# Two weight chunks of the first projection group are split on ScalarE and VectorE instead of GpSimd

## The reference

```
x = x + sincos_2d(SEQ)
sh1, sc1, gt1, sh2, sc2, gt2 = adaln(c, ada_w, ada_b)         # silu(c) @ ada_w + ada_b, also for c_ctx
hc = modulate(rms_norm(ctx, norm1_g), csh1, csc1)             # h * (1 + scale) + shift
hx = modulate(rms_norm(x, norm1_g), sh1, sc1)
... = hx @ w_in, hc @ w_in                                    # 12 chunks of 512 columns
```

## Time and profile before

| | |
|---|---|
| median of 3 runs | 2148.82 us (2142.51 to 2149.39) |
| profiled execution, span from first to last instruction | 2142.0 us |
| TensorE busy (matmul) | 2005.6 us, 94% |
| VectorE busy | 724.0 us, 34% |
| ScalarE busy | 594.7 us, 28% |
| GpSimd busy | 385.9 us, 18% |
| mean granted TensorE clock | 0.964 of full |
| loaded from HBM | 426.07 MB, 199 GB/s over the span |

### The profile page before, as it was taken

How to read it: one execution, slowest core, us unless ns; L and a number is a source line. 1 busy time by engine, 2 the same in 40 slices (tenths; PEclk the granted TensorE clock), 3 DMA queues, 4 the chain that set the end, 5 groups by cost and what they waited for, 6 DMA issues and landing times.

```text
span 2142.0 us, 27488 instructions
## 1 busy us (share of the span) xinstructions
PE 2005.6 (94%) x11518; PEld 1431.7 (67%) x11518; DVE 724.0 (34%) x1201; ACT 594.7 (28%) x921; POOL 385.9 (18%) x183
## 2 busy tenths in 40 slices
PE   7799989999999999998999798999999899889998
PEld 2567787775444444446887646777777678579998
DVE  1523154323222222226343614222222535533333
ACT  2413112022222222223113414222332311534443
POOL 2400000000000000005003012333343010414653
PEclk9899978989999999999999899999999999998999
DMA  9268914447999999982224003344334232413450
GB/s 358 96 244 295 369 51 160 160 158 305 425 428 419 426 421 427 423 358 105 100 79 150 1 30 138 138 143 171 137 137 140 78 106 94 157 52 145 158 187 29
DMA packets 120207, 428.28 MB, mean 200 GB/s; under 512 B 5690, under 2 KB 23141, under 8 KB 107456
## 3 DMA queue, kind: packets, MB, share of 16 engines
q1 hardware_dynamic: 118016, 416.56, 50.5%
q0 software_dynamic: 2112, 10.57, 1.4%
HBM read 426.07 MB, written 1.05 MB: 199 GB/s over the span
## 4 chain that ended last, share of the span: by engine, by line
PE 70%; PEld 5%; DVE 4%; issue 3%; ACT 3%; POOL 2%; PEldq 0%; DVEq 0%; ACTq 0%
PE bank L505 68%; PEld bank L505 5%; PE bank L520 1%; DVE H L1805 0%; DVE X L2344 0%; POOL arena L1723 0%; POOL arena L1722 0%; DVE arena L2288 0%; POOL arena L1727 0%; PEldq L494 0%; POOL arena L1725 0%; DVE H_low L1812 0%; POOL arena L1728 0%; DVE H L2260 0%; DVE ring_low L2158 0%
## 5 line engine op out<-in xcount | busy, mean ns | idle before, releaser
L505 PE MATMUL bank<-arena_r 128*128 128x512 f32 (+1 forms) x1920 | 560.7, 357 | 40.3 <-DVE H_low L1812 20.8
L505 PE MATMUL bank<-arena_r,ring_low 128*128 128x512 f32 (+2 forms) x1792 | 567.0, 349 | 20.5 <-DVE H_low L1812 17.5
L505 PEld LDWEIGHTS bank<-arena_r 128*128 128x128 f32 x1920 | 342.9, 192 | 138.9 <-issue 56.0
L505 PEld LDWEIGHTS bank<-arena_r,ring_low 128*128 128x128 f32 (+1 forms) x1792 | 333.5, 191 | 67.5 <-issue 21.8
L505 PE MATMUL bank<-arena 128*128 128x64 bf16 (+9 forms) x2684 | 329.3, 291 | 24.7 <-DMA arena<-in_hy_filt_w 11.9
L505 PEld LDWEIGHTS bank<-arena 128*128 128x128 bf16 (+4 forms) x2684 | 210.5, 141 | 128.1 <-issue 90.9
L505 PE MATMUL bank<-ring,arena 128*64 128x512 f32 x1024 | 278.2, 595 | 1.1 <-ACT arena L1423 0.7
L2344 DVE SCALAR_TENSOR_TENSOR X<-bank,mod,X 128x256 f32<-128x256 f32 x216 | 96.4, 481 | 394.0 <-PE bank L505 394.0
L505 PE MATMUL bank<-H_low,arena_r 128*128 128x512 f32 (+1 forms) x608 | 208.0, 342 | 0.0
L1749 POOL TENSOR_TENSOR ring_low<-ring,arena_r 128x2048 fp32r<-128x2048 f32 x32 | 146.6, 4603 | 118.5 <-ACT arena_r L1611 118.5
L1271 ACT ACTIVATE arena<-bank 128x512 f32<-128x512 f32 (+2 forms) x106 | 52.4, 496 | 413.5 <-PE bank L505 413.2
(11 more groups left out here) (263 smaller groups left out, 1908.0 us busy)
## 6 DMA issues: line engine op xcount, KB each, us to landing
ring<-in_moe_w_gate SPq DMA_DIRECT2D x32, 2048.0 KB, 13.7
ring<-in_w_mlp SPq DMA_DIRECT2D x32, 2048.0 KB, 8.3
ring<-in_w_in SPq DMA_DIRECT2D x26, 2048.0 KB, 8.8
ring<-in_ada_w SPq DMA_DIRECT2D x24, 2048.0 KB, 11.8
ring<-in_moe_w_up SPq DMA_DIRECT2D x17, 2048.0 KB, 9.2
H<-in_moe_w_down SPq DMA_DIRECT2D x16, 2048.0 KB, 16.1
arena<-in_moe_w_up SPq DMA_DIRECT2D x15, 2048.0 KB, 9.5
ring<-in_moe_w_down SPq DMA_DIRECT2D x15, 2048.0 KB, 16.3
```

Of the source, the lines that this page charges most:

```text
L505: ins = nc.tensor.matmul(o, l, r, start=start, stop=stop, skip_group_check=True)
```

## The change

GpSimd no longer splits anything in the first phase. Chunk win(0): ScalarE makes the high half in two copies of 2048 columns, after `ada_rows(2)` and before `ada_rows(3)`, and raises `first_high`; VectorE makes the low half in two subtractions, after `take_chunk(0, 2)` and before `take_chunk(0, 3)`, and raises `first_low`, for which TensorE waits at k = 0 and 4. Chunk win(1): VectorE splits it with `split_first(1)`, whole, at the start of the phase "projected", that is after the norm; TensorE waits for it before j = 1. The other edits renumber what is counted on `pool_ready` and `w_split`.

```diff
--- before.py
+++ after.py
@@ -617,10 +617,8 @@
 
                 wide = 2 * L if c in (1, 2) else L
                 if j < 4:
-                    if j == 1:
-                        pe.wait_ge(S("pool_ready"), 8)
-                    elif j:
-                        pe.wait_ge(S("w_split"), j - 1)
+                    if j:
+                        pe.wait_ge(S("w_split"), j)
                     wh, wl = W0h[j % 2].rearrange("p (k n) -> p k n", k=KT), as_cols(n, slot=low)
                 else:
                     chunk_in(n)
@@ -629,7 +627,7 @@
                     for k in range(KT):
                         pe.wait_ge(S("h_split"), k + 1)
                         if k % 4 == 0:
-                            pe.wait_ge(S("pool_ready"), 2 + k // 2)
+                            pe.wait_ge(S("first_low"), k // 4 + 1)
                         for nt in range(2):
                             t = slice(nt * P, (nt + 1) * P)
                             mm3(o[nt], (wh[:, k, t], wl[:, k, t]), (Hp[:, k, :], Hl[:, k, :]), k == 0, k == KT - 1,
@@ -894,7 +892,7 @@
                     for tb in range(TB):
                         mm(ps[2 * tb + nb], PICK[:, tb * P:(tb + 1) * P], YSl[:, s], False, False)
 
-            pe.wait_ge(S("pool_ready"), 9)
+            pe.wait_ge(S("pool_ready"), 1)
             pe.wait_ge(S("onehot"), 1)
             gather(0, 7, "gathered")
             pe.wait_ge(S("hg_ready"), 1)
@@ -950,7 +948,7 @@
                 pe.wait_ge(S("squares"), 8 * 3 + k + 1)
                 mm(ps[0][:, 0:L], ones, H[:, k, 0:L], k == 0, k == KT - 1)
                 if k == 0:
-                    pe.wait_ge(S("pool_ready"), 10)
+                    pe.wait_ge(S("pool_ready"), 2)
                 mm(ps[1][:, 0:L], FIN2[:, k, :], H[:, k, 0:L], k == 0, k == KT - 1, "sum_ready" if k == KT - 1 else None)
             phase_end(pe, "experts")
 
@@ -1193,7 +1191,7 @@
                             for a in range(2):
                                 ada(n, 7 + i, 7, 2 * u + a, 4, ADA_COLS, turns)
                                 n += 1
-                        pe.wait_ge(S("w_split"), 2 + 8 * l + j + 1)
+                        pe.wait_ge(S("w_split"), 3 + 8 * l + j + 1)
 
                         for nt, ks in [(0, (0, 1, 2)), (1, (0, 1, 2)), (0, (3,)), (1, (3,))] + [(t, (0, 1, 2, 3)) for t in range(2, KT)]:
                             if ks[0] == 0:
@@ -1293,8 +1291,14 @@
             mean_root(0, 2 * L, 4, RS0)
             act.wait_ge(S("lb_arg"), 1)
             A_(lbc[:, 8:24], lbc[:, 8:24], ACT.Exp).then_inc(S("lb_exp"), 1)
-            for i in range(1, 4):
+            for i in range(1, 3):
                 ada_rows(i, 6 + i % 2, i % 2)
+            n = win(0)
+            act.wait_ge(full[n % RING], arrived(n))
+            for a in range(2):
+                s = slice(2048 * a, 2048 * (a + 1))
+                A_(W0h[0][:, s], slot(n)[:, s], ACT.Copy).then_inc(S("first_high"), 1)
+            ada_rows(3, 7, 1)
             for k in range(KT):
                 done[0] += 2
                 act.wait_ge(S("scaled"), done[0])
@@ -1672,16 +1676,6 @@
             bring(A3(0, KT, L), tall(T["pos"]), "x_in")
             bring(X[:, :, L:2 * L], tall(T["ctx"]), "x_in")
             bring(A(15360, 4096), T["hy"], "tables_in")
-            for j in range(2):
-                n = win(j)
-                pool.wait_ge(full[n % RING], arrived(n))
-                if j:
-                    pool.wait_ge(S("filt_mm"), 8)
-                for a in range(2):
-                    s = slice(2048 * a, 2048 * (a + 1))
-                    G.tensor_copy(W0h[j][:, s], slot(n)[:, s]).then_inc(S("pool_ready"), 1)
-                    pool.wait_ge(S("pool_ready"), 4 * j + 2 * a + 1)
-                    G.tensor_tensor(low(n)[:, s], slot(n)[:, s], W0h[j][:, s].bitcast(F32), ALU.subtract).then_inc(S("pool_ready"), 1)
             phase_end(pool, "filters")
             pool.wait_ge(S("tile_done"), 16)
             bring(hmask, T["hg_mask"].rearrange("p (a b) -> p a b", a=2), "x_in")
@@ -1705,7 +1699,7 @@
             pool.wait_ge(full[L0 % RING], arrived(L0))
             pool.wait_ge(used, L0 + 1 - RING + 1)
             G.tensor_copy(low(L0 + 1), slot(L0)).then_inc(S("pool_ready"), 1)
-            pool.wait_ge(S("pool_ready"), 11)
+            pool.wait_ge(S("pool_ready"), 3)
             G.tensor_tensor(low(L0), slot(L0), low(L0 + 1).bitcast(F32), ALU.subtract).then_inc(full[(L0 + 1) % RING], 16)
             phase_end(pool, "experts")
             bring(b2t, T["b2"], "b2_in")
@@ -1874,6 +1868,11 @@
             take_chunk(0, 1, 7, 4)
             decayed(1)
             take_chunk(0, 2, 6, 8)
+            n = win(0)
+            for a in range(2):
+                s = slice(2048 * a, 2048 * (a + 1))
+                dve.wait_ge(S("first_high"), a + 1)
+                V.tensor_tensor(low(n)[:, s], slot(n)[:, s], W0h[0][:, s].bitcast(F32), ALU.subtract).then_inc(S("first_low"), 1)
             take_chunk(0, 3, 7, 12)
             dve.wait_ge(S("base_in"), 16)
             dve.wait_ge(S("ada_out"), 2 + 4)
@@ -1925,8 +1924,9 @@
                 link(V.tensor_tensor(QD, QD, Qt, ALU.mult))
 
             for j in range(8):
-                if j in (1, 2):
-                    dve.wait_ge(S("tile_done"), 4 * j)
+                if j < 3:
+                    if j:
+                        dve.wait_ge(S("tile_done"), 4 * j)
                     split_first(j + 1)
                 if j == 4:
                     dve.wait_ge(S("tile_done"), 16)
```

## The result

The changed kernel took 2130.4 us (median of 4 runs, 2128.6 to 2131.35), the one before 2148.4 beside it: ratio 0.9925, 95% interval 0.9909 to 0.9941, which is 16.1 us, with 12.7 to 19.6 as the interval. The medians themselves are 18.0 us apart, and 18.9 in a second comparison (e8: 2128.0 against 2146.9, ratio 0.9916, 0.9903 to 0.9929). The forecast was 2132.8, a gain of 16.0.

What follows compares the result with a forecast made beforehand. TensorE bounds the kernel nearly everywhere, idling 13.84 us before j=0 for VectorE. Gap 13.7 plus clock 2.3 gives 16.0 us: span 2142.0 to 2126.0, plus 6.8 for the median, 2132.8 us; own range 2127 to 2137, wider 2124 to 2140.5.

Steps and rivals of the forecast that it cites:

- The gap before j=0 is VectorE held by GpSimd's instructions: TensorE's 13.84 us idle before projection group j=0: GpSimd's SBUF reads exclude VectorE's two-input norm instructions; gain 13.7 us.
- Rival 3: Stall before j=0 isn't GpSimd's: h_split 1 stays at 76.5, gain 0, time 2148.8 us; chance 0.03.
- Two copies on ScalarE, 1.84 each, two subtractions on VectorE, 2.2 each, for nothing: Splitting win(0) before the norm: ScalarE's copies fit 0.8 us of slack; VectorE's take_chunk(0, 3) moves by 0.2.
- Rival 2: win(0)'s landing now holds ScalarE and VectorE queues: costs if after 50.3; at 71, 7 us slower, 2156; chance 0.03.
- j=0 starts at 62.8: First projection group starts when TensorE's own queue is free after spectrum(1), at 62.8 instead of 76.50: 13.7 us gained.
- The norm keeps its lead; h_split 8 at 71.6: First half of j=0: VectorE's norm starts 3.4 us ahead; TensorE reaches k=7 at 72.3, 0.7 us after h_split 8.
- wrong tight points: Norm's lead over TensorE in j=0: said to be 0.7 us at k=7, with 1.2 at the tightest earlier point, k=4.
- Rival 1: First half of j=0: VectorE 2 to 5 us slower holds TensorE; gain 9 to 14, 2135 to 2140; chance 0.14.
- 2.3 us by the clock: Group j=0: without the gap TensorE stays at 2.4 GHz, so 24.3 us shrinks, gaining 2.3 more if it never stands.
- the gain would be 13.7 alone: Whole change: without any effect of the clock, only the 13.7 us of the gap before j=0 would be gained.
- win(1) hidden, shift kept: VectorE's split of win(1) ends at 79.3, over 5 us to spare before j=1; later loads shift along, nothing taken back.
- Rival 4: TensorE's later waits: shifted clock stretches take the gain back, leaving under 6.4 us, time about 2145; chance 0.05.

Runs made afterwards that it cites:

- e8: The changed kernel run and profiled once more, nothing altered: 2128.0 us against 2146.9 for the kernel before, ratio 0.9916.
- e1: Only win(0) moved to ScalarE and VectorE, GpSimd still splitting win(1), against the kernel before: 2143.5 us, ratio 0.9980.
- e2: Only win(1) moved to VectorE after the norm, GpSimd still splitting win(0), against the kernel before: 2135.4 us, ratio 0.9941.
- e3: Changed kernel plus GpSimd copies and subtractions on an unused area that nobody waits for: 2148.0 us, 1.0004 of the kernel before.
- e4: Changed kernel plus sixteen GpSimd zero fills of an unused area, writing without reading: 2131.0 us, 0.9927 of the kernel before.
- e6: Changed kernel plus one VectorE subtraction of 2048 columns right before the norm: 2133.8 us, 0.9945 of the kernel before.
- e5: Kernel before, with fifteen matmuls of constants filling TensorE's idle gap before j=0: 2146.5 us, ratio 0.9999.
- e9: Changed kernel, but TensorE begins j=0 only when the whole norm is finished: 2140.5 us, 0.9976 of the kernel before.

## Why the prediction was right, point by point

- *The gap before j=0 is VectorE held by GpSimd's instructions.* Right, and shown three ways: e1 and e2 bring back each stretch of the stall with the part of GpSimd's work that lies over it, and e3 brings all of it back with idle work. Rival 3 is dead. That a reading instruction is needed was a rule when I wrote; in e4 writing ones leave the norm alone.
- *Two copies on ScalarE, 1.84 each, two subtractions on VectorE, 2.2 each, for nothing.* 3.71 and 4.48 us for the pairs; `ada_rows(3)` still had to wait for TensorE, and `gains` began at 56.07 as forecast. Rival 2 (the landing in two queues) never came near.
- *j=0 starts at 62.8.* It was 61.94; e8 has 62.52. From the start of `spectrum(1)` it is 7.38 us (54.56 to 61.94), against 7.25 in my sum. What differs is that start, 55.55 in the first profile of the kernel before; in the eleven others it lies anywhere from 54.52 to 55.39, 54.90 in the second profile of the kernel before, so it is scatter. In the changed kernel's profile `ada(3)` ran at full clock (1.93 us at 51.01), as in e3 and e4; in the others it took 3.2 to 3.6. The gap itself shrank by 13.58 us, forecast 13.7.
- *The norm keeps its lead; h_split 8 at 71.6.* Its last pair ended at 70.6; my sum gave the last step a `scale` pair that it hasn't (1.06 us, not 1.59), and had the first pair 0.4 late. The lead at the start was 2.9, not 3.4. I also named the wrong tight points: by my own figures the lead is 1.4 at k=4 and 0.9 at k=6, and in the trace it was smallest at k=6, 0.6. Rival 1 (the norm paces TensorE) did not come, but by less than the prediction let one think: with 1.3 us less lead it costs 0.8 us (e6), and in e2, where the norm has no lead and the clock is low at first, 2.4.
- *2.3 us by the clock.* The size was right (j=0 is 2.4 us shorter), the cause was only half of it. I took the ten slow matmuls for the whole of the lost time and overlooked my own number: at 1.59 us per k the norm would have held even a quick TensorE for just as long. e5 gives the clock back and gains 0.0; e9 takes it away where the norm leads and loses 1.76. So the 2.4 us need both, a norm that leads when TensorE arrives and a clock that hasn't fallen, and the change brings both. The sum came out because both readings are differences to the same 21.9 us. My sentence that without any effect of the clock the gain would be 13.7 alone was wrong: had the clock not fallen before, as in e5, j=0 would have been as long, and the change would have gained the same 16.
- *win(1) hidden, shift kept.* Both right: 7 us to spare, 5.13 before j=2, the rest unchanged. Rival 4 is there only as scatter, some 3 us up and down in the rest, seen in the kernel before (2041.1 and 2044.9) and among the runs that change only this stage; that the clock makes it was not tested. The 14.16 us that I gave for the blocks of the expert stage isn't the 14.33 of the earlier trace rows; nothing in the sum hangs on it.

## What to carry to other kernels

If GpSimd reads SBUF beside a long row of short VectorE instructions with two inputs from SBUF, price each GpSimd instruction as a stop of VectorE for its whole length, not by the share of time that GpSimd is busy; moving 25.9 us of GpSimd's work onto the busier VectorE and ScalarE gained 16 here. Instructions that only write cost the norm nothing (e4). When an engine follows another step by step, find out which of the two is slower at full speed before crediting a clock: the clock is worth something only where TensorE isn't held by the other engine anyway (0.0 us in e5, 1.76 in e9). And check the difference of two profiled spans with a second pair when it is below 1%.

## What the runs showed that I had not expected

- The exclusion is mutual, and in most rows the start decides: a GpSimd CAST or COPY of 2048 columns took 3.44 and 3.83 us beside VectorE (e1, e3) against 1.89; `gains` took 1.90 us when it began 0.02 us behind a GpSimd CAST (56.00 against 55.98) and 0.18 when it began 0.02 before one (e2). The exception is e1's first CAST, which began between VectorE instructions and let four of them pass.
- GpSimd's fills (e4) left 32 norm instructions at 0.47 us, but a TENSOR_SCALAR of 8 columns took 1.73.
- The same matmuls at 1.2 GHz for 4.5 us and at 2.4 GHz throughout took the same 24.36 us, because they followed the norm (before, e5).
